# Statistics moved into feed-forward steps, one modulation pass in eight moved from VectorE to ScalarE, and x loaded in two transfers

## The chip, the cores and the metric

The kernel runs on one core of a Trainium2 chip. The metric is the device time of one launch in microseconds, as the median of several runs. The program is one long chain of dense layers for 256 tokens of 1024 features; nothing is shared with another core.

## The reference, cut to what matters

Two blocks of two layers each are applied one after the other. The first block is attention in three branches and a feed-forward part; the second is modulated by a condition vector `c`.

```python
# first block, each of two layers
h = rmsnorm(x, norm_mlp_g[l])
x = x + jnp.square(jax.nn.relu(h @ w_up[l])) @ w_down[l]      # 1024 -> 4096 -> 1024
...
# second block, each of two layers
mod = silu(c) @ ada_w[l] + ada_b[l]                           # 1024 x 9216, one row
sh1, sc1, g1, sh2, sc2, g2, sh3, sc3, g3 = jnp.split(mod, 9, axis=-1)
```

`rmsnorm` divides a row by the root of its mean square. The `mod` row of the second block depends on `c` alone, so it can be computed at any time before that block; the kernel computes it during the feed-forward parts of the first block.

## The kernel before, in words

Every large product is done in fp32 split in two parts: a rounded "high" part and the rest, "low". Three matmuls (lines 603, 604 and 605: high by high, low by high, high by low) make one product. Weights come in chunks of 1 MB (128 x 2048 fp32) from one stream, loaded by SyncE's queue into three raw slots. For each chunk ScalarE writes the high part in two halves (lines 383 and 384) and VectorE the low part in two halves (line 405), into one of two buffers. A raw slot is free again when the low part is done; one of the two split buffers when TensorE has used the chunk before the last.

**Start.** x comes in one transfer. ScalarE squares and sums it in four pieces (line 465), adds EPS (467) and takes ln and exp (469, 470) for each of the two token tiles; VectorE scales x by the result (478), TensorE turns it (491), ScalarE and VectorE make the high and low parts of h (543, 553), and the first product starts. In between the first weight chunk is split, both high halves on ScalarE.

**Feed-forward part of a first-block layer.** There are 16 steps. TensorE runs up0, up1, dn0, up2, dn1, ... (48 matmuls of 256 columns for an up chunk, 24 of 512 columns for a down chunk). In step j ScalarE waits until up j is done, splits the next chunk's high part (dn0 in step 0, up j+1 later), applies relu (1382) and square (1386), splits dn j once dn j-1 is used, copies the hidden rows' high part (696), and issues the two modulation transfers 2j+4 and 2j+5 (`ada_load(j + 2)`, line 1226, 1152 KB each, on ScalarE's own queue). VectorE does the low parts of the same chunks, the hidden rows' low part (702), and two modulation passes, `mac(2j + 2)` and `mac(2j + 3)`. The engines take their instructions strictly in the order written.

**Modulation.** The 1024 x 9216 weight is read as 32 slots (four quarters of 8 slots of 128 x 2304). `mac(i)` multiplies slot i by one condition value per partition and adds it to the quarter's accumulator (1517); the first slot of a quarter (i = 0, 8, 16, 24) writes it instead (1514). Four slot buffers are used in turn. So slot 8 is transferred after step 2 issues it and used by VectorE in step 3, slot 16 is issued in step 6 and slot 24 in step 10.

**Statistics of the second norm.** Since relu and square commute with a positive row scale, the norm's scale is applied only when the feed-forward sum is added to x. The four `norm_square` calls (squares of x in four pieces) stand ahead of step 0 in ScalarE's order; their results are used after step 15.

Of the kernel before, what the change touches and what calls it, by code (L numbers as in the profile page):

```python
# [19 lines left out]
ACT = mybir.ActivationFunctionType  # L20
ALU = mybir.AluOpType
# [4 lines left out]
D = 1024  # L26
# [4 lines left out]
SPLIT = 1024  # L31
# [77 lines left out]
PIECES_OUT = ((0, 0), (1, 0), (0, 1), (1, 1))  # L109
# [107 lines left out]
for _n, _w in (("norm", 24), ("ada_b", MOD), ("dqk", 2), ("dout", 1), ("conv_w", 62), ("conv_b", 2), ("cng", 2), ("cnb", 2), ("fqk", 2)):  # L217
# [14 lines left out]
    "key_rope_ready", "lam_exp", "lam_sum", "latent_rstd", "ln_rstd", "ln_stat", "mac_done", "mix_high", "mix_low",  # L232
    "eps_ready", "softplus_done", "rg_log", "gate_ready", "fgate_log", "conv_log",
    "mla_exp", "mla_masked", "mla_p", "mla_rope_ready", "mla_top", "mods_ready", "o_ready", "o_sq", "p_ready",
# [6 lines left out]
class Machine:  # L241


    def __init__(self, nc):
# [29 lines left out]

        self.loaded = [nc.alloc_semaphore(f"input_loaded{i}") for i in range(9)]
        self.raw_full = [nc.alloc_semaphore(f"raw_full{s}") for s in range(RAW)]
# [524 lines left out]
def ada_acc(m, q):  # L801
    return m.work[:, (q % 2) * ADA_W:(q % 2 + 1) * ADA_W]
# [410 lines left out]
def act_layer1(act, m, plan, step, ada):  # L1213
# [10 lines left out]
    def ada_load(j):  # L1224
        for i in (2 * j, 2 * j + 1):
            act.dma_start(ada_slot(m, i), ada[l * 32 + i]).then_inc(m.ada_full[i % 4], 16)

    def g1(name, t):
        at = l * NV1 + VEC1[name][0] + t
        return m.vec1[:, at:at + 1]  # L1230

    if l == 0:
        split_high(act, m, plan, 0)
        act.wait_ge(m.loaded[2], 16)
    norm_high(act, m, plan, 0, "n1", lambda t: g1("mix", t))
    split_high(act, m, plan, 1)
    if l == 0:
# [133 lines left out]
    for t in range(KT):  # L1371
        if t == 4:
            at_event(split_high, act, m, plan, "wc3")
        high_plain(act, m, plan, "n2", t, g1("mlp", t))
    for i in range(4):
        norm_square(act, m, step, 0, PIECES_OUT, i, -1.0)
    for j in range(FF_TILES):
# [15 lines left out]
        if j + 2 < FF_TILES:  # L1393
            act.wait_ge(m["mac_done"], 32 * l + 2 * j + 2)
            ada_load(j + 2)
    split_high(act, m, plan.next, 0)
    for i in range(4):
# [3 lines left out]
def vec_layer1(dve, m, plan, step):  # L1401
# [102 lines left out]
    def mac(i):  # L1504

        q, kt = i // 8, i % 8
        dve.wait_ge(m.ada_full[i % 4], l * 128 + (16 * (i // 4) + 16))
        ck = m.small[:, 32 + kt:33 + kt]
        if kt == 0:
            if q >= 2:  # L1510
                m.wait_full(dve, plan, f"ada{q - 2}")
            elif l > 0:
                dve.wait_ge(m["ada_last"], l)
            dve.tensor_scalar(ada_acc(m, q), ada_slot(m, i), ck, None, ALU.mult).then_inc(m["mac_done"], 1)
        else:
            dve.wait_ge(m["mac_done"], 32 * l + i)
            dve.scalar_tensor_tensor(ada_acc(m, q), ada_slot(m, i), ck, ada_acc(m, q), ALU.mult, ALU.add).then_inc(m["mac_done"], 1)  # L1517

# [1142 lines left out]
def vec_setup(dve, m):  # L2661
    dve.memset(m.small[:, 0:1], EPS).then_inc(m["eps_ready"], 1)
    norm_unit(dve, m, 0, 0)
    norm_unit(dve, m, 0, 1)


# [32 lines left out]
def act_setup(act, m, step):  # L2699
    act.preload_act_table_set("natural_log_exp_and_others")  # L2700
    act.wait_ge(m.loaded[0], 16)
    act.wait_ge(m["eps_ready"], 1)
    for i in range(4):
        norm_square(act, m, step, None, PIECES_DOWN, i)

# [36 lines left out]
def build(nc, x, pos, c, consts, vec1, vec2, final, row2, stream1, stream2, ada, out):  # L2742
    m = Machine(nc)
    with nc.Block() as block:

        @block.sync
        def _(sp):
            for s in range(RAW):
                sp.sem_inc(m.raw_done[s], 2)
            ident, late = P, CONST["freq"][0]  # L2750
            sp.dma_start(m.x[:, :], x).then_inc(m.loaded[0], 16)
            sp.dma_start(m.consts[:, 0:ident], consts[:, 0:ident]).then_inc(m.loaded[1], 16)
            sp.dma_start(m.vec1[:, :], vec1).then_inc(m.loaded[2], 16)
            for plan in PLANS1 + PLANS2:
# [243 lines left out]
```

## Time and profile before

| what | value |
|---|---|
| median of 3 runs | 2006.41 us (2005.88 to 2006.75) |
| profiled execution | 2007.09 us, span 2004.3 us |
| TensorE busy | 1952.3 us, 97% of the span |
| VectorE busy | 1444.8 us, 72% |
| ScalarE busy | 1148.6 us, 57% |
| DMA | 409.55 MB, mean 204 GB/s |
| first modulation pass of a quarter, line 1514 on VectorE | 8 times, 1.416 us each |
| first weight chunk, from issue at 2.31 us to landing | 6.6 us |
| first up2 matmul, second layer | 799.42 us; last up1 matmul starts at 792.44 us |
| first up4 matmul, second layer | 822.01 us |

The span is what the profiler saw of one execution; the execution's own time is 2.8 us longer. Idle time of ScalarE or VectorE costs nothing while TensorE goes on; a time is lost only where TensorE stops.

### The profile page before, as it was taken

To read this page: it belongs to the slowest core of one execution; us is meant where nothing else is said; L and a number is where in the kernel's file an instruction comes from. 1 tells how busy PE (TensorE), PEld (TensorE's weight loads), DVE (VectorE), ACT (ScalarE), POOL (GpSimd) and SP (SyncE) were. 2 spreads that over 40 slices of the span, in tenths; PEclk is the share of its full clock that TensorE was granted. 3 is DMA by queue.
4 is the path that set the end of the run, shared out by engine and by line. 5 is a ranking of instruction groups with operands and counts; after the bars stand their busy time and mean duration, and the time that the engine had idled before them with its cause. 6 is when DMAs were issued, how large, how long until landed. Compare 5 with 4: busy or idle time off the path is not lost.

```text
span 2004.3 us, 33258 instructions
## 1 busy us (share of the span) xinstructions
PE 1952.3 (97%) x13792; PEld 1761.0 (88%) x13792; DVE 1444.8 (72%) x1922; ACT 1148.6 (57%) x1814; POOL 43.4 (2%) x32
## 2 busy tenths in 40 slices
PE   7999999999999999999899999999999999999999
PEld 7898888888989898888799988699989998878998
DVE  5756798888565788988756589765576657977555
ACT  6358845455436865454655566755565556566554
POOL 0100000000010000000000000000000100000000
PEclk9999999999999999999999999999999999999999
DMA  7453378996554356999455542365546554334553
GB/s 275 144 210 107 125 265 326 389 386 245 194 189 149 105 176 267 391 388 374 167 187 189 189 158 96 107 205 185 184 154 213 189 187 151 126 127 151 188 187 126
DMA packets 56164, 409.55 MB, mean 204 GB/s; under 512 B 6608, under 2 KB 6992, under 8 KB 7888
## 3 DMA queue, kind: packets, MB, share of 16 engines
q1 hardware_dynamic: 46512, 330.23, 46.5%
q10 hardware_dynamic: 9504, 77.21, 9.5%
q8 instruction: 109, 1.79, 0.3%
q14 instruction: 39, 0.32, 0.0%
HBM read 406.37 MB, written 1.05 MB: 203 GB/s over the span
## 4 chain that ended last, share of the span: by engine, by line
PE 79%; DVE 14%; ACT 5%; issue 2%; DMA 0%; DVEq 0%; ACTq 0%; SPq 0%
PE bank L603 25%; PE bank L605 24%; PE bank L604 24%; DVE weights_low L405 4%; ACT weights_high L383 1%; DVE work L2417 1%; DVE work L1517 1%; DVE scratch L1445 1%; ACT work L465 1%; PE bank L940 1%; DVE work L566 1%; DVE h_low L572 1%; ACT weights_high L384 0%; DVE work L1607 0%; DVE scratch L1602 0%
## 5 line engine op out<-in xcount | busy, mean ns | idle before, releaser
L405 DVE TENSOR_TENSOR weights_low<-raw_weights,weights_high 128x1024 fp32r<-128x1024 f32 x608 | 728.4, 1237 | 364.2 <-ACT weights_high L383 357.2
L603 PE MATMUL bank<-h_high,weights_high 128*128 128x256 f32 x3024 | 857.7, 284 | 15.0 <-DVE h_low L572 11.1
L605 PE MATMUL bank<-h_high,weights_low 128*128 128x256 f32 x3024 | 845.3, 280 | 0.0
L604 PE MATMUL bank<-h_low,weights_high 128*128 128x256 f32 x3024 | 844.7, 279 | 0.0
L383 ACT ACTIVATE weights_high<-raw_weights 128x1024 fp32r<-128x1024 f32 x296 | 313.4, 1059 | 619.6 <-PE bank L605 587.9
L603 PEld LDWEIGHTS bank<-h_high,weights_high 128*128 128x128 f32 x3024 | 567.9, 188 | 36.7 <-issue 17.0
L604 PEld LDWEIGHTS bank<-h_low,weights_high 128*128 128x128 f32 x3024 | 568.4, 188 | 2.9 <-issue 0.5
L605 PEld LDWEIGHTS bank<-h_high,weights_low 128*128 128x128 f32 x3024 | 568.6, 188 | 0.0
L384 ACT ACTIVATE weights_high<-raw_weights 128x1024 fp32r<-128x1024 f32 x296 | 309.0, 1044 | 0.0
L603 PE MATMUL bank<-weights_high,hidden_high 128*128 128x512 f32 x640 | 254.3, 397 | 5.1 <-DVE work L2491 2.9
L605 PE MATMUL bank<-weights_high,hidden_low 128*128 128x512 f32 x640 | 252.7, 395 | 0.0
L604 PE MATMUL bank<-weights_low,hidden_high 128*128 128x512 f32 x640 | 252.7, 395 | 0.0
L603 PEld LDWEIGHTS bank<-weights_high,hidden_high 128*128 128x128 f32 x640 | 120.0, 188 | 33.4 <-ACT work L2296 3.3
L1517 DVE SCALAR_TENSOR_TENSOR work<-work,small 128x2304 f32<-128x2304 f32 x56 | 146.5, 2616 | 3.5 <-DVE work L1517 0.5
L605 PEld LDWEIGHTS bank<-weights_high,hidden_low 128*128 128x128 f32 x640 | 120.0, 188 | 29.4
L604 PEld LDWEIGHTS bank<-weights_low,hidden_high 128*128 128x128 f32 x640 | 120.0, 188 | 26.1 <-issue 0.5
L603 PE MATMUL bank<-weights_high,h_high 128*128 128x256 f32 (+1 forms) x320 | 102.9, 322 | 1.0 <-DVE h_low L1178 0.7
L604 PE MATMUL bank<-weights_low,h_high 128*128 128x256 f32 (+1 forms) x320 | 100.7, 315 | 0.0
L605 PE MATMUL bank<-weights_high,h_low 128*128 128x256 f32 (+1 forms) x320 | 100.6, 314 | 0.0
L455 DVE SCALAR_TENSOR_TENSOR work<-bank,work 128x512 f32<-128x512 f32 x74 | 51.1, 691 | 31.2 <-ACT work L449 31.2
L603 PEld LDWEIGHTS bank<-weights_high,h_high 128*128 128x128 f32 x320 | 60.6, 189 | 9.3 <-issue 5.2
L605 PEld LDWEIGHTS bank<-weights_high,h_low 128*128 128x128 f32 x320 | 60.8, 190 | 4.4
(304 smaller groups left out, 1880.0 us busy)
## 6 DMA issues: line engine op xcount, KB each, us to landing
raw_weights<-in_stream SPq DMA_DIRECT2D x310, 1024.0 KB, 4.9
work<-in_ada ACTq DMA_DIRECT2D x64, 1152.0 KB, 9.4
consts<-in_consts SPq DMA_DIRECT2D x1, 2048.0 KB, 12.2
work<-in_row ACTq DMA_DIRECT2D x2, 836.0 KB, 5.5
x<-in_x SPq DMA_DIRECT2D x1, 1024.0 KB, 4.9
out_x<-x SPq DMA_DIRECT2D x4, 256.0 KB, 2.0
gain_row<-in_final SPq DMA_DIRECT2D x1, 512.0 KB, 12.8
vec<-in_vec SPq DMA_DIRECT2D x1, 169.0 KB, 12.1
```

Source lines behind the costliest of these rows:

```text
L383: act.activation(high[:, 0:SPLIT], raw[:, 0:SPLIT], ACT.Copy).then_inc(m["high_a"], 1)
L384: act.activation(high[:, SPLIT:CH], raw[:, SPLIT:CH], ACT.Copy).then_inc(m["high_b"], 1)
L405: dve.tensor_tensor(low[:, c], raw[:, c], high[:, c].bitcast(F32), ALU.subtract).then_inc(m.raw_done[plan.index[name] % RAW], 1)
L455: return dve.scalar_tensor_tensor(to, z, 0.0, to, ALU.min, ALU.subtract)
L465: step(act.activation(h_temp(m)[:, c], m.x[:, c], ACT.Square, accum_out=stat(m, tt, 0 if first else 1)))
L566: dve.tensor_scalar(modulated(m, t), z, gain(t), shift(t), ALU.mult, ALU.add).then_inc(m["temp_vec"], 1)
L572: dve.tensor_tensor(m.hL[:, c], modulated(m, t), m.hH[:, c].bitcast(F32), ALU.subtract).then_inc(m["h_ready"], 1)
L603: pe.matmul(out, aH, bH, start=start, stop=False, skip_group_check=True)
L604: pe.matmul(out, aH, bL, start=False, stop=False, skip_group_check=True)
L605: return pe.matmul(out, aL, bH, start=False, stop=stop, skip_group_check=True)
L940: pe.matmul(m.ps[7][r, c:c + 256], v[:, h * 64:h * 64 + 64], a[:, 0:256], start=True, stop=False, skip_group_check=True)
L1517: dve.scalar_tensor_tensor(ada_acc(m, q), ada_slot(m, i), ck, ada_acc(m, q), ALU.mult, ALU.add).then_inc(m["mac_done"], 1)
```

## The change

There are three edits. First, the start: x is loaded as two transfers of 512 KB, one for each token tile, with the identity matrix's transfer between them, and the first high half of the first weight chunk is made by VectorE (line 2683 of the new kernel, a copy) after it has scaled x; ScalarE makes the second half only. Second, the four `norm_square` calls stand at the ends of steps 2, 3, 4 and 5. Third, the writing pass of the quarters 1 to 3 (slots 8, 16 and 24) is made by ScalarE, at the ends of steps 2, 6 and 10, right behind the transfer that it reads; VectorE waits for it and goes on with the next slot.

```diff
+    def mac_first(q):
+        act.wait_ge(m.ada_full[(8 * q) % 4], l * 128 + 16 * (2 * q) + 16)
+        if q >= 2:
+            m.wait_full(act, plan, f"ada{q - 2}")
+        act.activation(ada_acc(m, q), ada_slot(m, 8 * q), ACT.Copy, scale=m.small[:, 32:33]).then_inc(m["mac_first"], 1)
...
     if l == 0:
-        split_high(act, m, plan, 0)
+        m.wait_raw(act, plan, plan.split[0])
+        split_high_half(act, m, plan, 0, 1)
         act.wait_ge(m.loaded[2], 16)
     norm_high(act, m, plan, 0, "n1", lambda t: g1("mix", t))
+    if l == 0:
+        m.wait_split_first(act, plan, plan.split[0])
...
-    for i in range(4):
-        norm_square(act, m, step, 0, PIECES_OUT, i, -1.0)
     for j in range(FF_TILES):
...
             ada_load(j + 2)
+        if 2 <= j < 6:
+            norm_square(act, m, step, 0, PIECES_OUT, j - 2, -1.0)
+        if j % 4 == 2 and j < 12:
+            mac_first(j // 4 + 1)
...
-        if kt == 0:
-            if q >= 2:
-                m.wait_full(dve, plan, f"ada{q - 2}")
-            elif l > 0:
+        if i == 0:
+            if l > 0:
                 dve.wait_ge(m["ada_last"], l)
             dve.tensor_scalar(ada_acc(m, q), ada_slot(m, i), ck, None, ALU.mult).then_inc(m["mac_done"], 1)
+        elif kt == 0:
+            dve.wait_ge(m["mac_first"], 3 * l + q)
         else:
-            dve.wait_ge(m["mac_done"], 32 * l + i)
-            dve.scalar_tensor_tensor(ada_acc(m, q), ada_slot(m, i), ck, ada_acc(m, q), ALU.mult, ALU.add).then_inc(m["mac_done"], 1)
+            if kt > 1 or i == 1:
+                dve.wait_ge(m["mac_done"], 32 * l + i)
+            dve.scalar_tensor_tensor(ada_acc(m, q), ada_slot(m, i), ck, ada_acc(m, q), ALU.mult,
+                                     ALU.add).then_inc(m["mac_done"], 2 if kt == 1 and q > 0 else 1)
...
 def vec_setup(dve, m):
     dve.memset(m.small[:, 0:1], EPS).then_inc(m["eps_ready"], 1)
+    dve.wait_ge(m.loaded[0], 16)
     norm_unit(dve, m, 0, 0)
+    dve.wait_ge(m.loaded[9], 16)
     norm_unit(dve, m, 0, 1)
+    first, name = PLANS1[0], PLANS1[0].split[0]
+    m.wait_raw(dve, first, name)
+    dve.tensor_copy(m.halves(first, name)[0][:, 0:SPLIT], m.raw_slot(first, name)[:, 0:SPLIT]).then_inc(m["high_a"], 1)
...
-            sp.dma_start(m.x[:, :], x).then_inc(m.loaded[0], 16)
+            sp.dma_start(m.x[:, 0:D], x[:, 0:D]).then_inc(m.loaded[0], 16)
             sp.dma_start(m.consts[:, 0:ident], consts[:, 0:ident]).then_inc(m.loaded[1], 16)
+            sp.dma_start(m.x[:, D:2 * D], x[:, D:2 * D]).then_inc(m.loaded[9], 16)
```

ScalarE, first layer, from the transfers that step 2 issues to the first instructions of step 3, before:

```order
L1226 DMA work<-in_ada 128x2304 [waits mac_done]
L1226 DMA work<-in_ada 128x2304
L383 ACTIVATE weights_high<-raw_weights 128x1024 [waits bank_full2,raw_full1]
L384 ACTIVATE weights_high<-raw_weights 128x1024
L1382 ACTIVATE work<-bank 128x512
```

and now, where `ada_full0` is the landing of slot 8:

```order
L1226 DMA work<-in_ada 128x2304 [waits mac_done]
L1226 DMA work<-in_ada 128x2304
L465 ACTIVATE work,small<-x 128x512 [waits x_ready]
L467 ACTIVATE small<-small 128x1 [waits act_step]
L1233 ACTIVATE work<-work,small 128x2304 [waits ada_full0,act_step]
L383 ACTIVATE weights_high<-raw_weights 128x1024 [waits bank_full2,raw_full1]
```

Three instructions stand ahead of the split of up4 (the L383 that waits for up3's bank) that were not there, and the last of them waits for a transfer issued four rows above it.

ScalarE, first layer, between the h parts and step 0, before (the statistics, then the split of dn0):

```order
L543 ACTIVATE h_high<-bank,vec 128x256 [waits bank_full2] x2
L465 ACTIVATE work,small<-x 128x512 [waits x_ready]
L467 ACTIVATE small<-small 128x1 [waits act_step]
L465 ACTIVATE work,small<-x 128x512 [waits x_ready,act_step]
L467 ACTIVATE small<-small 128x1 [waits act_step]
L465 ACTIVATE work,small<-x 128x512 [waits x_ready,act_step]
L469 ACTIVATE small<-small 128x1 [waits act_step]
L470 ACTIVATE small<-small 128x1 [waits act_step]
L465 ACTIVATE work,small<-x 128x512 [waits x_ready]
L469 ACTIVATE small<-small 128x1 [waits act_step]
L470 ACTIVATE small<-small 128x1 [waits act_step]
L383 ACTIVATE weights_high<-raw_weights 128x1024 [waits bank_full3,raw_full2]
```

and now:

```order
L543 ACTIVATE h_high<-bank,vec 128x256 [waits bank_full2] x2
L383 ACTIVATE weights_high<-raw_weights 128x1024 [waits bank_full3,raw_full2]
L384 ACTIVATE weights_high<-raw_weights 128x1024
L1390 ACTIVATE work<-bank 128x512
L1394 ACTIVATE work<-work 128x512 [waits act_freed]
```

The ten instructions of the statistics are gone from this place, and the split of dn0 follows the last h part.

VectorE at the start, now:

```order
L478 TENSOR_SCALAR work<-x,small 128x512 [waits rstd_ready,input_loaded0]
L478 TENSOR_SCALAR work<-x,small 128x512
L478 TENSOR_SCALAR work<-x,small 128x512 [waits rstd_ready,input_loaded9]
L478 TENSOR_SCALAR work<-x,small 128x512
L2683 CAST weights_high<-raw_weights 128x1024 [waits raw_full0]
L405 TENSOR_TENSOR weights_low<-raw_weights,weights_high 128x1024 [waits high_a]
L553 SCALAR_TENSOR_TENSOR h_low<-bank,vec,h_high 128x256 [waits hH_ready,bank_full0,input_loaded2]
```

The CAST is the added row; without it the rows are those of before.

## Rows read from the trace of the kernel before

**Rows 1.** The page's chain that ended last, shares of the span by engine.
```profile
PE 79%; DVE 14%; ACT 5%; issue 2%; DMA 0%; DVEq 0%; ACTq 0%; SPq 0%
```

**Rows 2.** Timeline, all engines, start: start us, duration us, engine, line, operation.
```profile
0.93 0.39 SPq L2751 DMA_DIRECT2D x<-in_x  x1
...
10.26 0.20 ACT L470 ACTIVATE small<-small 128x1 f32<-128x1 f32 x1
...
10.50 0.88 DVE L478 TENSOR_SCALAR work<-x,small 128x512 f32<-128x512 f32 x2 [1.37 <-ACT small L470]
...
11.45 1.23 DVE L405 TENSOR_TENSOR weights_low<-raw_weights,weights_high 128x1024 fp32r<-128x1024 f32 x1
...
13.23 1.66 DVE L553 SCALAR_TENSOR_TENSOR h_low<-bank,vec,h_high 128x256 fp32r<-128x256 f32 x4 [0.56 <-ACT h_high L543]
14.16 0.29 PEld L603 LDWEIGHTS bank<-h_high,weights_high 128*128 128x128 f32 x1 [1.55 <-DVE h_low L553]
...
17.74 0.41 PE L604 MATMUL bank<-h_low,weights_high 128*128 128x256 f32 x1
```

**Rows 3.** The page's DMA issues: count, KB each, median us from issue to landing.
```profile
work<-in_ada ACTq DMA_DIRECT2D x64, 1152.0 KB, 9.4
...
x<-in_x SPq DMA_DIRECT2D x1, 1024.0 KB, 4.9
out_x<-x SPq DMA_DIRECT2D x4, 256.0 KB, 2.0
```

**Rows 4.** Timeline of TensorE, first layer, feed-forward steps 1 to 3.
```profile
313.92 0.28 PE L605 MATMUL bank<-h_high,weights_low 128*128 128x256 f32 x1
...
321.17 0.36 PE L603 MATMUL bank<-h_high,weights_high 128*128 128x256 f32 x1 [0.62 <-DVE weights_low L405]
...
338.16 0.40 PE L603 MATMUL bank<-weights_high,hidden_high 128*128 128x512 f32 x1
...
343.76 0.28 PE L603 MATMUL bank<-h_high,weights_high 128*128 128x256 f32 x1
```

**Rows 5.** Timeline of ScalarE, first layer, feed-forward steps 0 and 3.
```profile
310.11 1.04 ACT L383 ACTIVATE weights_high<-raw_weights 128x1024 fp32r<-128x1024 f32 x1
...
338.44 1.06 ACT L383 ACTIVATE weights_high<-raw_weights 128x1024 fp32r<-128x1024 f32 x1 [3.13 <-PE bank L605]
```

**Rows 6.** Timeline of VectorE, first layer, feed-forward steps 0 and 1.
```profile
311.26 2.36 DVE L405 TENSOR_TENSOR weights_low<-raw_weights,weights_high 128x1024 fp32r<-128x1024 f32 x2 [3.40 <-ACT weights_high L383]
...
314.56 5.33 DVE L1517 SCALAR_TENSOR_TENSOR work<-work,small 128x2304 f32<-128x2304 f32 x2
319.81 4.62 DVE L405 TENSOR_TENSOR weights_low<-raw_weights,weights_high 128x1024 fp32r<-128x1024 f32 x4
```

**Rows 7.** Line 1226, step 2 of the first layer: the pair's issues and landings.
```profile
L1226 ACTq DMA_DIRECT2D work<-in_ada x2: 334/395/456, 332.9 to 333.3; - x2
...
DMA to landing us min/median/max: 8.6/10.7/12.8
```

**Rows 8.** The page's groups of ScalarE copies: busy us, mean ns of one.
```profile
L384 ACT ACTIVATE weights_high<-raw_weights 128x1024 fp32r<-128x1024 f32 x296 | 309.0, 1044 | 0.0
```

**Rows 9.** ScalarE's groups by shape: busy us, mean ns.
```profile
L696 ACT ACTIVATE hidden_high<-work 128x512 fp32r<-128x512 f32 x76 | 46.8, 616 | 0.1
```

**Rows 10.** Line 1226, step 2 of the second layer.
```profile
L1226 ACTq DMA_DIRECT2D work<-in_ada x2: 335/395/455, 811.2 to 811.5; - x2
...
DMA to landing us min/median/max: 8.4/10.6/12.7
```

**Rows 11.** Line 1226, step 6 of the first layer.
```profile
L1226 ACTq DMA_DIRECT2D work<-in_ada x2: 334/395/456, 379.2 to 379.6; - x2
...
DMA to landing us min/median/max: 6.8/9.3/11.7
```

**Rows 12.** Timeline of TensorE, first layer: the first matmul of up8.
```profile
390.36 0.28 PE L603 MATMUL bank<-h_high,weights_high 128*128 128x256 f32 x1
```

**Rows 13.** Busy time by stretch: PE, PEld, DVE, ACT, POOL, PEclk, DMA share, GB/s.
```profile
324.00:468.00 144.00, 143.93 (x948) 126.85 (x947) 125.81 (x92) 69.60 (x86) 0.00 (x0) 1.00 0.97 388
```

More of the change, by code:

```diff
@@ L232 @@
     "key_rope_ready", "lam_exp", "lam_sum", "latent_rstd", "ln_rstd", "ln_stat", "mac_done", "mix_high", "mix_low",
-    "eps_ready", "softplus_done", "rg_log", "gate_ready", "fgate_log", "conv_log",
+    "eps_ready", "mac_first", "softplus_done", "rg_log", "gate_ready", "fgate_log", "conv_log",
     "mla_exp", "mla_masked", "mla_p", "mla_rope_ready", "mla_top", "mods_ready", "o_ready", "o_sq", "p_ready",
@@ L272, in __init__ @@
         self.ps = [nc.alloc_psum_tensor(f"bank{b}", [P, 512], F32) for b in range(8)]
-        self.loaded = [nc.alloc_semaphore(f"input_loaded{i}") for i in range(9)]
+        self.loaded = [nc.alloc_semaphore(f"input_loaded{i}") for i in range(10)]
         self.raw_full = [nc.alloc_semaphore(f"raw_full{s}") for s in range(RAW)]
@@ L2703, in act_setup @@
     for i in range(4):
+        if i == 2:
+            act.wait_ge(m.loaded[9], 16)
         norm_square(act, m, step, None, PIECES_DOWN, i)
```

## The prediction

> **What bounds the kernel now.** I read the chain of waits first. It gives TensorE 79% of the span and VectorE 14% [rows 1], so a gain has to come from a place where TensorE stands still, and a loss arises where a new wait reaches it. The timeline of TensorE shows two such places beside the change. At the start it has nothing to do with products until 14.16 [rows 2]. In the feed-forward part of the first layer it ends up1 at 313.92 + 0.12 = 314.04, and starts up2 only at 321.17, released by VectorE's low part [rows 4]. An undisturbed down chunk takes 343.76 - 338.16 = 5.60, and up4 follows dn2 there without a gap [rows 4]. The reader is to see that in step 3 there is no wait to remove, but a seam that can open. The third view is the pair of transfers that each step issues: it lands 8.6 us or more after its issue in step 2 [rows 7], in a stretch where the DMA engines are busy 0.97 of the time [rows 13].
>
> **The statistics leave the place before step 0.** Before, ScalarE started the split of dn0 at 310.11 [rows 5], straight behind the four squares. Its own release is the end of up0. An up chunk takes 5.65 (ScalarE's step of 11.25 less 5.60), so up1 began near 308.4, and ScalarE starts 0.28 after such a seam (338.44 against 338.16, [rows 4, 5]): 308.7. ScalarE, and VectorE behind it, come 1.4 earlier. VectorE's passes stand from 314.56 to 319.81, then the low part of up2, and TensorE follows 321.17 - 319.81 = 1.36 later [rows 4, 6]. Now that is 318.4 + 1.36 = 319.8; TensorE itself would be ready at 314.04 + 5.60 = 319.64. up2 starts at 319.8 instead of 321.17: 1.4 gained. The second layer has the same seam, up1 ending at 792.56 and up2 starting at 799.42. TensorE is ready at 798.16, so at most 1.26 is gained, and VectorE is advanced by about as much. Together **-2.65**. Once VectorE is earlier, the next thing late is TensorE's own dn0.
>
> The squares themselves land in steps 2 to 5. One piece with its small operations is about 1.2 us (four took the 4.5 us between the h parts and 310.11) and ScalarE idled 3.13 before step 3's split [rows 5]. They cost nothing in steps 3 to 5. In step 2 they are covered by the wait that comes next.
>
> **The writing pass on ScalarE.** VectorE loses six passes of 1.416 us, in steps 3, 7 and 11. TensorE did not wait for VectorE in these steps (up4 followed dn2 without a gap), so this saves nothing. What the pass costs on ScalarE has no row of its size. From 128x512 in 0.616 to 128x1024 in 1.044 [rows 8, 9] is 0.84 ns an element, and 1.044 + 1280 x 0.00084 = 2.1; in proportion to the larger one it would be 2.25 x 1.044 = 2.35, and at the rate of the slope alone 1.9. I take 2.1, by the row nearest in size, and keep 1.9 to 2.35.
>
> More important is when it can start. It waits for slot 8, whose transfer is issued four rows earlier, and the split of up4 is queued behind it on ScalarE. For that split VectorE's low part waits, and for that TensorE. In the first layer the pair is issued at 332.9 and the first of it lands 8.6 later, at 341.5 [rows 7]. The pass then runs to 343.65. The split of up4, which started at 338.44, starts there. From the start of a high half to VectorE's low half is 311.26 - 310.11 = 1.15 [rows 5, 6], from there to TensorE 1.36. TensorE gets up4 at 343.65 + 2.5 = 346.15 instead of 343.76: **+2.4**. All this moves as a whole by the 1.4 gained before. In the second layer the issue at 811.2 and the landing 8.4 later [rows 10] give 819.6 + 2.1 + 2.5 = 824.2 against 822.01: **+2.2**.
>
> In step 6 the pair is issued at 379.2 and slot 16 lands 6.8 later, at 386.0 [rows 11]; 386.0 + 2.1 + 2.5 = 390.6 against 390.36 [rows 12]: **+0.3**. Step 6 of the second layer and step 10 of both have landings of 5.2 to 6.6, and come out at or before TensorE's own time: 0. The transfers that step 3 issues go out later by what TensorE was held, and they are used later by as much, so I count nothing more. Sum of the waits: **+4.9**.
>
> On these transfers the Trainium skill (DMA: Bandwidth & Descriptors, Issuing engines are not separate DMA queues) says that transfers started by different engines share the same 16 DMA engines and interleave. The trace agrees: 1152 KB need 8.6 us here. This page speaks against the third edit, as ScalarE's own queue gives the slot no right of way over the weights.
>
> **The start.** x in one piece lands 4.9 after its issue, 256 KB of the output take 2.0 [rows 3]. Between them, 512 KB would take 2.97, which is 1.9 less; at the rate of the busiest stretches, about 430 GB/s, half of x is 1.2 less. I take 1.4. ScalarE needs the second half 2.4 us after its start, when by its place in the queue it has landed. Everything down to VectorE's second scaling then moves from 10.50 to 9.1. ScalarE then makes one weight half instead of two and is no longer last; VectorE is, as it has the copy too. Its low half started at 11.45 and the first low part of h at 13.23, 0.56 of that waiting for ScalarE [rows 2]. This wait goes, and the copy comes in. The copy has no row of its own. The scaling of 128x512 takes 0.44 of VectorE's time (0.88 for two), the subtraction of the same 128x1024 takes 1.23 [rows 2]. At twice the scaling less one start it is about 0.7, at the subtraction 1.2. With 0.7, VectorE's first low part starts at 13.23 - 1.4 + (0.7 - 0.56) = 12.0, TensorE gains about 1.3; with 1.2 it gains 0.8. I take 0.7 since it too reads one tensor: **-1.3**. Bounds 0.5 and 1.9. The first weight chunk lands at 2.31 + 6.6 = 8.9, in time for either.
>
> For the copy the Trainium skill (VectorE: DVE Perf Modes, The perf-mode tier table) says that fp32 copies and tensor-scalar operations in SBUF run at twice the rate of an fp32 operation on two tensors. The scaling rows agree; that it holds for a copy with a rounded output no row of before shows. By the rule the start gives -1.3, by the subtraction's row -0.8.
>
> **The sum.** -2.65 + 4.9 - 1.3 = +0.95 against the profiled execution's 2007.09, which is 2008.0. The median of the runs is 2006.41, 0.68 lower, so the forecast for it is 2007.4, which is no change: a measurement of this kernel can tell about 0.2%, 4 us, from nothing.
>
> **The rivals.**
>
> *Slow landings.* The slot lands as late in steps 6 and 10 as the median of all 64 transfers, 9.4 us [rows 3]. For: the median itself, and a DMA share of 0.97 [rows 13]. Against: the pair's second half makes that median, the first one came after 5.2 to 8.6 in all six places. Its place is ScalarE before the split of up8 and up12. Price at 9.4: step 2 costs 3.2 in each layer, and the four others about 2.8 each (379.2 + 9.4 + 4.6 = 393.2 against 390.36). That is 6.4 + 11.2 = 17.6, less 2.65 and 1.3: +13.7, or 2020. It decides from landings of 7.4 in the four later places on: then these cost 4 x 0.8 = 3.2, the waits are 4.6 + 3.2 = 7.8, and the sum is 7.8 - 3.95 = +3.9, or 2010.3.
>
> *No wait at all.* If the slot lands within 6.2 us of its issue in step 2, as it does in later steps, the pass ends in ScalarE's idle time. For: 5.2 to 6.8 elsewhere. Against: 8.6 and 8.4 at the very place [rows 7, 10]. Then -2.65 - 1.3 = -3.95, or 2002.4.
>
> *The start gives little.* Either TensorE's clock rises at the same time as before, or the copy is slow. Until 17.74 a matmul of 256 columns is shown with 0.41 [rows 2], later with 0.28 [rows 4], starting 0.21 and 0.12 apart: TensorE is at its 1.2 GHz level at first and then at 2.4. If it rises at the same time, half of the 1.3 is lost. Result 2006.41 + 0.95 + 0.65 = 2008.0.
>
> *VectorE sets the end of a step.* If the six passes taken from VectorE were on its path after all, 6 x 1.416 = 8.5 would be gained, or 1999. Only steps 3, 7 and 11 could show it, and TensorE's seams there are closed before. I give it almost nothing.
>
> **How the numbers follow.** The forecast 50%, the start giving little 19%, slow landings 17% (half of them between 2010 and 2012), no wait 12%, VectorE 2%. The predicted time is 2007.4. The no-wait case lies on the edge of what can be told; with the larger start gain of 1.9 it is beyond it, and I count 9 of its 12 as faster, with VectorE's 2. The range reaches into the no-wait case down to 2003.0, and into slow landings up to 2011.5 (7.7 us in the later places). Faster than 2002.4: 11%; slower than 2010.4: 17%; in between 72%.
>
> **What would show it.** Right: TensorE reaches the first product at about 12.9; up2 follows dn0 without a gap in both layers; in step 2 ScalarE sits idle for some 4 to 5 us ahead of the 128x2304 pass, released by the transfer, and TensorE then waits about 2.3 us before up4, released by VectorE's low part; before up8 and up12 it waits 0.3 or less. Wrong: no such wait before up4; the wait before up8 or up12 over 1 us; a stop before dn4 or later for a transfer that step 3 issued late; or a start that comes no earlier.

## The result, and the profile after

The changed kernel takes 2012.94 us in the median (2007.05 to 2019.46, 16 runs) against 2006.58 (2003.70 to 2009.13, 16 runs) for the kernel before on the same chip. The ratio is 1.0033, 95% interval 1.0023 to 1.0043: some 6.6 us slower, above the forecast's range of 2003.0 to 2011.5. The 16 runs lie in two groups of eight, 2007.05 to 2011.47 and 2014.41 to 2019.46, and the median falls between them. The profiled execution took 2017.55 us with a span of 2015.4, so it is one of the slower ones; a second profiled execution of the same kernel took 2012.71 (below, changed again).

The page's chain of waits gives TensorE 77% instead of 79% [rows 1], and the DMAs, which had 0%, now hold 3%:

```profile
PE 77%; DVE 13%; ACT 4%; DMA 3%; issue 2%; SPq 0%; DVEq 0%; ACTq 0%
```

**Statistics.** The timeline of TensorE at up2, first layer (start us, duration us, then engine, line and operation), answers to [rows 4]:

```profile
317.74 0.40 PE L605 MATMUL bank<-weights_high,hidden_low 128*128 128x512 f32 x1
318.08 0.36 PE L603 MATMUL bank<-h_high,weights_high 128*128 128x256 f32 x1
```

The gap before up2 is gone. A seam is the place where one chunk's matmuls end and the next chunk's begin. "Cost at a seam" means, all along this document, how much further one matmul lags behind its twin in the trace of before than the matmul ahead of it did. From the last matmul of up1 to the first of up2 it was 321.17 - 313.92 = 7.25 before; now up1's last starts at 312.26, and it is 318.08 - 312.26 = 5.82. TensorE gains 1.43, and in the second layer 0.95.

**The writing pass.** ScalarE between steps 2 and 3, first layer, same columns; in brackets its idle time before an instruction and what ended it. The L1226 row is the issue of the two transfers:

```profile
330.10 1.06 ACT L383 ACTIVATE weights_high<-raw_weights 128x1024 fp32r<-128x1024 f32 x1 [2.85 <-DMA raw_weights<-in_stream]
330.19 0.82 ACTq L1226 DMA_DIRECT2D work<-in_ada  x2
...
333.27 0.29 ACT L467 ACTIVATE small<-small 128x1 f32<-128x1 f32 x1
339.53 2.22 ACT L1233 ACTIVATE work<-work,small 128x2304 f32<-128x2304 f32 x1 [5.96 <-DMA work<-in_ada]
341.66 1.04 ACT L383 ACTIVATE weights_high<-raw_weights 128x1024 fp32r<-128x1024 f32 x1
```

and line 1226 there, which answers to [rows 7]:

```profile
DMA to landing us min/median/max: 9.3/11.8/14.3
```

The pass takes 2.22, within the 1.9 to 2.35 that was kept for it. The slot lands 9.3 after its issue, not 8.6. TensorE, in the same place:

```profile
340.43 0.40 PE L605 MATMUL bank<-weights_high,hidden_low 128*128 128x512 f32 x1
344.17 0.36 PE L603 MATMUL bank<-h_high,weights_high 128*128 128x256 f32 x1 [3.34 <-ACT work L1390]
344.36 0.28 PE L604 MATMUL bank<-h_low,weights_high 128*128 128x256 f32 x1
344.48 0.28 PE L605 MATMUL bank<-h_high,weights_low 128*128 128x256 f32 x1
...
345.74 0.42 PE L603 MATMUL bank<-h_high,weights_high 128*128 128x256 f32 x1
345.96 0.42 PE L604 MATMUL bank<-h_low,weights_high 128*128 128x256 f32 x1
...
348.92 0.28 PE L603 MATMUL bank<-h_high,weights_high 128*128 128x256 f32 x1
349.04 0.28 PE L604 MATMUL bank<-h_low,weights_high 128*128 128x256 f32 x1
```

Read the starts, not the durations. The stop before up4 costs 3.50. The profile says that ScalarE's relu of up3's bank ended it (L1390, at 344.12); VectorE's first low half of up4, begun at 342.80, ends within 0.2 of that, and behind the stop of up8 it is the one that is named. Then the matmuls start 0.12 apart, from 345.53 to 348.74 they start 0.21 apart, and after that 0.12 again. In 3.4 us TensorE does 16 matmuls where 0.117 each would have taken 1.9: **1.5 us more, behind the stop**. The view of busy time by stretch shows why (its column after POOL is the granted clock, then DMA share and GB/s):

```profile
344.20:348.70 4.50, 4.50 (x26) 4.50 (x27) 3.89 (x5) 3.91 (x7) 0.00 (x0) 0.64 0.65 215
...
395.30:399.80 4.50, 4.50 (x26) 4.50 (x27) 3.89 (x5) 3.01 (x4) 0.00 (x0) 0.65 0.67 227
```

The granted clock is 0.64 there and was 1.00 before the stop: TensorE falls from its 2.4 GHz level to the 1.2 GHz level for some 3.4 us. The second of these rows is up8. There ScalarE's pass, whose landing answers to [rows 11]:

```profile
390.64 2.22 ACT L1233 ACTIVATE work<-work,small 128x2304 f32<-128x2304 f32 x1 [7.26 <-DMA work<-in_ada]
```

and TensorE, the first matmul of up8 answering to [rows 12]:

```profile
391.89 0.40 PE L605 MATMUL bank<-weights_high,hidden_low 128*128 128x512 f32 x1
395.28 0.36 PE L603 MATMUL bank<-h_high,weights_high 128*128 128x256 f32 x1 [3.00 <-DVE weights_low L405]
```

The slot, issued at 381.0, landed 9.6 later instead of the 6.8 of before. The stop costs 3.1 and the slow matmuls 1.6. Before up4 of the second layer the stop is 3.2 and the slow matmuls 1.5; up8 there costs nothing, up12 0 in the first layer and 0.3 in the second. So three seams cost 5.0 + 4.7 + 4.7 = 14.4, where the forecast had 4.9 in all.

**The start**, all engines, answers to [rows 2]:

```profile
4.55 0.63 ACT L465 ACTIVATE work<-x 128x512 f32<-128x512 f32 x1 [2.53 <-DMA x<-in_x]
7.28 0.63 ACT L465 ACTIVATE work<-x 128x512 f32<-128x512 f32 x1 [0.36 <-DMA x<-in_x]
9.75 0.88 DVE L478 TENSOR_SCALAR work<-x,small 128x512 f32<-128x512 f32 x2 [1.84 <-ACT small L470]
10.55 0.69 DVE L2683 CAST weights_high<-raw_weights 128x1024 fp32r<-128x1024 f32 x1
12.41 1.65 DVE L553 SCALAR_TENSOR_TENSOR h_low<-bank,vec,h_high 128x256 fp32r<-128x256 f32 x4
13.34 0.58 PE L603 MATMUL bank<-h_high,weights_high 128*128 128x256 f32 x1 [1.08 <-DVE h_low L553]
```

The first product comes 0.82 earlier. The copy costs 0.69, as chosen. But ScalarE waits 0.36 for the second half of x, and VectorE's second scaling moves only from 10.50 to 9.75. TensorE's first matmuls start 0.21 apart and later ones 0.12. Once both kernels are at 0.12, from 17.77 on, the gain is 0.66. The moment of this rise is not the same in every execution. In the second profiled execution of the changed kernel the first product is 0.70 earlier than in the trace of before and only 0.16 is left after the rise; in the kernel without the third edit 0.81 and 0.07. With the start of before unaltered (the statistics alone, the third edit alone) the rise came so early that those two executions were 1.8 ahead of the trace of before.

### The profile page after: what moved, and what is told of

Read it like the earlier page. It is cut to its first block, busy times and chain, and to the rows that moved or that the text cites. A ratio compares the mean times of both kernels' runs of the same rounds, so it can differ in the third digit from the quotient of the medians.

```text
span 2015.4 us, 33268 instructions
## 1 busy us (share of the span) xinstructions
PE 1954.8 (97%) x13792; PEld 1762.4 (87%) x13792; DVE 1436.6 (71%) x1917; ACT 1160.4 (58%) x1819; POOL 41.1 (2%) x32
## 4 chain that ended last, share of the span: by engine, by line
PE 77%; DVE 13%; ACT 4%; DMA 3%; issue 2%; SPq 0%; DVEq 0%; ACTq 0%
PE bank L603 24%; PE bank L605 24%; PE bank L604 23%; DVE weights_low L405 4%; DMA work<-in_ada 1%; ACT weights_high L383 1%; DMA raw_weights<-in_stream 1%; DVE work L2431 1%; DVE scratch L1457 1%; DVE work L1530 1%; PE bank L940 1%; DVE work L566 1%; DVE h_low L572 1%; DVE work L1621 0%; DVE scratch L1616 0%
## 5 line engine op out<-in xcount | busy, mean ns | idle before, releaser
L383 ACT ACTIVATE weights_high<-raw_weights 128x1024 fp32r<-128x1024 f32 x295 | 312.1, 1058 | 586.9 <-PE bank L605 553.6
```

Of the source, the lines that this page charges most:

```text
L383: act.activation(high[:, 0:SPLIT], raw[:, 0:SPLIT], ACT.Copy).then_inc(m["high_a"], 1)
```

## The experiments

Several accounts stood against each other. Mine: the third edit alone is the loss, through a stop that the late slot and the pass make together, and through the fall of the clock behind it. The rivals: that the other two edits do harm, that one half of the third suffices, or that the slow matmuls come from data that arrive slowly. Each ratio is to the kernel before on the same chip.

**Without the third edit.** VectorE's line 1514 makes all eight passes again, and `mac_first` is gone:

```diff
-        if j % 4 == 2 and j < 12:
-            mac_first(j // 4 + 1)
```

> The changed kernel with the writing pass back on VectorE (third edit undone; the start and the moved statistics stay). Theory A, the writing pass on ScalarE is the whole loss: it holds ScalarE until slot 8 has landed, TensorE stops about 3 us before up4 in each layer and sometimes before up8, and after such a stop it runs at its lower clock for some 4 us, which costs 1.5 us more. Then this kernel is 2 to 4 us faster than before (2002.5 to 2004.5) and its trace has no stop over 1 us before up4 or up8. Rival B, the moved statistics disturb steps 2 to 5: it stays 2 us or more slower than before. Rival C, the shifted start puts the DMA queues in a worse phase: no faster than before, with late landings.

Measured: 2003.48 (12 runs), ratio 0.9987 (0.9977 to 0.9996), so neither of the other two edits makes the loss. The last matmul of dn2 and the first of up4:

```profile
341.01 0.40 PE L605 MATMUL bank<-weights_high,hidden_low 128*128 128x512 f32 x1
341.24 0.28 PE L603 MATMUL bank<-h_high,weights_high 128*128 128x256 f32 x1
```

No stop. Up4 of the second layer costs 0.55.

**The third edit alone**, added to the kernel before.

> The kernel before with the third edit alone (writing pass of slots 8, 16, 24 on ScalarE). Theory A: 6 to 12 us slower than before (2012 to 2018), with stops of 2 to 3.5 us before up4 in both layers and slow matmuls behind those of 3 us and more. Rival B or C: within 2 us of before.

Measured: 2016.15 (7 runs), ratio 1.0041 (1.0026 to 1.0056). With the first run this puts the loss on the third edit. Its runs too lie in two groups, 2011.01 to 2012.19 and 2016.15 to 2016.69. Its first up4:

```profile
342.70 0.36 PE L603 MATMUL bank<-h_high,weights_high 128*128 128x256 f32 x1 [1.85 <-ACT work L1389]
...
343.77 0.41 PE L604 MATMUL bank<-h_low,weights_high 128*128 128x256 f32 x1
343.98 0.41 PE L605 MATMUL bank<-h_high,weights_low 128*128 128x256 f32 x1
```

The stops cost 2.0 and 2.2, and the clock falls behind both (+1.6, +1.5), where I had expected it behind stops of 3 and more only. Without the other two edits the stop is the 2.4 and 2.2 that I had worked out, or less.

**The pass one step later**, behind the square of steps 3, 7 and 11 of the changed kernel:

```diff
         act.activation(hidden(m, j), relu_temp(m, j), ACT.Square).then_inc(m["u_ready"], 1)
+        if j % 4 == 3 and j < 12:
+            mac_first(j // 4 + 1)
...
-        if j % 4 == 2 and j < 12:
-            mac_first(j // 4 + 1)
```

> The changed kernel with the writing pass on ScalarE one step later, behind the square of steps 3, 7 and 11, when ScalarE has already split the next up chunk. The pass is the same, only the wait for the landing no longer stands ahead of the split. Theory A: no stop before up4 and up8; 2 to 4 us faster than before, as without the pass on ScalarE (2002.5 to 2004.5). Rival D, the pass itself (2.2 us of ScalarE) or VectorE's wait for it is the cost: 4 us or more slower than that, 2007 or more.

Measured: 2003.77 (12 runs), ratio 0.9990 (0.9979 to 1.0001). ScalarE:

```profile
340.54 2.23 ACT L1233 ACTIVATE work<-work,small 128x2304 f32<-128x2304 f32 x1 [0.52 <-DMA work<-in_ada]
```

The same pass on the same engine costs TensorE nothing at the first layer's up4 and up8 and 0.65 at the second layer's up4. The place makes the loss.

**The wait alone**, on the kernel without the third edit: ScalarE waits for slots 8, 16 and 24 at the old place and does nothing with them.

```diff
+        if j % 4 == 2 and j < 12:
+            act.wait_ge(m.ada_full[0], l * 128 + 16 * (j + 2) // 2 + 16)
```

> The variant without the pass on ScalarE, but ScalarE still waits at the ends of steps 2, 6 and 10 until slot 8, 16 or 24 has landed; VectorE makes the pass. Theory A: the stop before up4 is that of the changed kernel less the pass, 3.3 - 2.1 = 1.2 us in both layers, without a fall of the clock; 2 to 4 us slower than the variant without pass (2005.5 to 2007.5). Rival F, the wait is nothing and the 2.2 us pass is what costs: as the variant without pass, 2003.5.

Measured: 2005.0 (11 runs), ratio 0.9989 (0.9980 to 0.9998). Up4 costs 0.1 in the first layer and 0.2 in the second. That is a miss: I had expected a stop of 1.2. In this execution the slot landed 8.3 after its issue; at the 9.3 of the changed kernel the wait would reach 1.0 further, and no trace of this kernel shows what that costs.

**The pass without the wait**, on the same kernel:

```diff
+        if j % 4 == 2 and j < 12:
+            step(act.activation(h_temp(m), m.x[:, :], ACT.Copy))
```

> The variant without the pass on ScalarE, but with a plain copy of 128x2048 on ScalarE at the ends of steps 2, 6 and 10 whose input has long been there (nothing reads it); VectorE makes the pass. Theory A: ScalarE idles over 3 us there, so no stop of TensorE and the same time as the variant without pass, within 1 us (2003.5). Rival F, the pass is what costs: 2 us or more slower.

The copy is 128x2048 and takes 1.94, a little less than the pass. Measured: 2004.26 (11 runs), ratio 0.9992 (0.9983 to 1.0001). No seam costs over 0.3. So in these executions ScalarE's idle time covers the wait alone, and it covers the work alone; one behind the other they are not covered.

**The start alone**, added to the kernel before.

> The kernel before with the new start alone. Theory A: the first product starts 0.6 to 0.9 us earlier as in the changed kernel, and this shift is still there at the end: 0 to 1.5 us faster than before, not to be told from no change. Rival G, the rest of the start is bound by the transfers or the clock: the shift is gone by 20 us.

Measured: 2007.77 (11 runs), ratio 1.0007 (0.9998 to 1.0016). The first product is at 13.59, 0.57 earlier, and 0.39 of it is left once the matmuls start 0.12 apart. The rival that nothing is left is not what this trace shows, but the time doesn't show a gain either.

**The statistics alone**, added to the kernel before.

> Before with the second edit alone: the four pieces of the statistics stand in steps 2 to 5, everything else is as before. By my term, up2 starts 1.3 to 1.4 us earlier in each layer and nothing else changes: 2.4 to 2.7 us less than before, ratio 0.9987. The rival that the chain absorbs it (VectorE's modulation passes set up2's low part anyway, so the split being earlier only lengthens a wait) gives no change, ratio 1.000. The rival that the squares in step 2 to 5 hold the next split of ScalarE gives a stop before up4 and a ratio above 1.

Measured: 2005.39 (11 runs), ratio 0.9985 (0.9976 to 0.9993). From up1's last matmul to up2's first TensorE gains 1.43 in the first layer and 1.15 in the second; up4 gives 0.36 and 0.14 back. Of the three edits alone, the product 0.9985 x 1.0007 x 1.0041 is 1.0033, the ratio of the whole; with intervals of 0.001 or so on each side, an agreement this close is partly chance.

**Stops of chosen length.** To the kernel before, unread copies of x on ScalarE at the ends of steps 2, 4, ... 12, longer from seam to seam in the first layer, shorter in the second. All transfers are there in time.

```diff
+        if j in DELAY[l]:
+            for n in DELAY[l][j]:
+                step(act.activation(h_temp(m)[:, 0:n], m.x[:, 0:n], ACT.Copy))
```

> The kernel before, with plain copies of x into a free scratch region added on ScalarE at the ends of steps 2, 4, 6, 8, 10 and 12 (nothing reads them), so long that TensorE should stop before the next up chunk for about 1.0, 1.5, 2.0, 2.5, 3.0 and 3.5 us, in this order in the first layer and in the reverse in the second. No transfer is waited for. Theory A with the clock: behind the long stops matmuls of 256 columns start 0.21 us apart for some 4 us, behind the short ones 0.12 from the first on; the changed kernel shows the fall after 3.3 us and the start of the second block shows none after 1.4, so the border lies between; it need not be sharp. Rival E, the slow matmuls come from late data: none of the twelve is followed by slow matmuls, as all its data are there.

One run, 2030.57. Cost of the stops at up4 to up14: 1.0, 0.8, 1.3, 1.6, 2.6, 2.7 in the first layer, none followed by slow matmuls; 3.5, 2.1, 2.5, 0.6, 1.1, 0.3 in the second, the first two followed by them (+1.6, +1.5). TensorE after the 3.5 and after the 2.1:

```profile
836.10 0.36 PE L603 MATMUL bank<-h_high,weights_high 128*128 128x256 f32 x1 [3.35 <-ACT work L1383]
...
863.53 0.35 PE L603 MATMUL bank<-h_high,weights_high 128*128 128x256 f32 x1 [1.84 <-ACT work L1383]
```

and the stretches behind these two and behind the 2.5:

```profile
836.10:840.50 4.40, 4.40 (x25) 4.40 (x26) 3.79 (x4) 3.04 (x4) 0.00 (x0) 0.64 0.58 203
...
863.60:868.00 4.40, 4.40 (x25) 4.40 (x26) 3.79 (x4) 2.97 (x4) 0.00 (x0) 0.62 0.65 226
...
890.20:894.60 4.40, 4.40 (x38) 4.40 (x39) 3.79 (x4) 2.97 (x4) 0.00 (x0) 1.00 0.66 216
```

With no late data the clock still falls, so slow data are not the cause. The border isn't sharp: the clock fell behind 2.1 and did not behind 2.5, 2.6 and 2.7. It is one execution.

**TensorE kept busy in the stop.** To the changed kernel, 26 matmuls (3.1 us) before up4 and up8 of both layers, into a bank that is overwritten.

```diff
+FILL = 26
...
+        if j in (4, 8):
+            pe_begin(pe, m, plan, f"up{j}")
+            for _ in range(FILL):
+                pe.matmul(m.bank(plan, f"up{j}")[:, 0:T], m.hH[:, 0:P], m.hH[:, 0:T], start=True, stop=True, skip_group_check=True)
```

> The changed kernel with 26 matmuls of 256 columns put into the seam before up4 and before up8 in both layers (about 3 us each; their result is overwritten). They need nothing that is late, so TensorE stays busy while it waits for the split. Theory A with the clock: the matmuls behind the seam before up4 start 0.12 us apart from the first on, and each stop of 3 us and more costs 1.5 us less than in the changed kernel, while a seam without a stop (up8 of the second layer) costs up to 3 us more: 0 to 4 us faster than the changed kernel's 2012.9 in all. Rival E, the slow matmuls behind the seam come from the data (the split arrives late in both halves) and not from the stop: they stay 0.21 us apart and nothing is gained.

Measured: 2016.58 (6 runs), ratio 1.0053 (1.0037 to 1.0069): a miss. The trace tells the two halves apart:

```profile
342.42 3.27 PE L1094 MATMUL bank<-h_high 128*128 128x256 f32 x26
345.92 0.36 PE L603 MATMUL bank<-h_high,weights_high 128*128 128x256 f32 x1 [0.23 <-ACT work L1395]
346.11 0.28 PE L604 MATMUL bank<-h_low,weights_high 128*128 128x256 f32 x1
346.23 0.28 PE L605 MATMUL bank<-h_high,weights_low 128*128 128x256 f32 x1
```

The clock stays up, but the fill costs its 3.1 also where there would have been no stop: up8 costs 3.1 in both layers, though slot 16 landed 5.3 after its issue in the first. A shorter one follows: 16 matmuls, before up4 of both layers and up8 of the first. Against the kernel just shown:

```diff
-FILL = 26
+FILL = 16
...
-        if j in (4, 8):
+        if j == 4 or (j == 8 and l == 0):
```

> The changed kernel with 16 matmuls of 256 columns, some 1.9 us, in front of up4 in both layers and of up8 in the first layer, where TensorE stands still for about 3.3 us. They write a bank that up4 or up8 overwrites, and run in time in which TensorE has nothing to do. If the clock's fall after a stop is what costs 1.5 us at each place, the rest of the stop is 1.4 us, the clock stays at its upper level, and the kernel is 3 to 4.5 us faster than the changed one: about 2008.5, ratio to before 1.001. If the filling takes as long as it gives (because it starts later than the stop does, as in the kernel with 26), the time is that of the changed kernel or above it, ratio 1.003 to 1.005. If the slow matmuls come from the work behind the stop and not from the stop, they stay, and the time is the changed kernel's.

Measured: 2012.67 (10 runs), ratio 1.0026 (1.0016 to 1.0035), which doesn't part from the changed kernel: a miss, as about 2008.5 was expected. The clock doesn't fall at the filled seams, where up4 costs 2.7 and 2.2. Up8's fill costs 1.9, since the slot landed 5.1 after its issue there and nothing would have stopped, and up12 of the second layer has a stop of 2.4 with a fall behind it (+1.6), as slot 24 landed 8.8 after its issue.

**The changed kernel again**, unaltered, one profiled run.

> The changed kernel once more, unaltered, for a second look at its three places. By the landings of the first look (9.3 and 9.6 us in steps 2 and 6) the stops are about 3.3 us each; if the landings scatter between executions, steps 2 and 6 land between 6.8 and 9.6, the stop before up4 lies between 2.2 and 3.5 and that before up8 between 0.3 and 3.2, and slow matmuls follow only where the stop is above about 2 us. A time between 2007 and 2019 is what either gives.

It took 2012.71. First-layer up4:

```profile
346.23 0.40 PE L603 MATMUL bank<-h_high,weights_high 128*128 128x256 f32 x1 [3.73 <-ACT work L1390]
346.43 0.41 PE L604 MATMUL bank<-h_low,weights_high 128*128 128x256 f32 x1
346.64 0.41 PE L605 MATMUL bank<-h_high,weights_low 128*128 128x256 f32 x1
```

and ScalarE's pass of step 6:

```profile
388.57 2.23 ACT L1233 ACTIVATE work<-work,small 128x2304 f32<-128x2304 f32 x1 [2.88 <-DMA work<-in_ada]
```

Up4 costs 3.9 + 1.55 and, in the second layer, 2.7 + 1.5. Up8 costs nothing: the pair was issued at 383.3, and the slot landed within 5.3. So up4 stops in both executions, and up8 (4.7) comes and goes with a landing.

**Fill before up4 alone**, 16 matmuls in both layers. Against the kernel with the short fill:

```diff
-        if j == 4 or (j == 8 and l == 0):
+        if j == 4:
```

> The changed kernel with 16 matmuls of 256 columns in front of up4 alone, in both layers; in front of up8 there are none, since the slot sometimes lands early there and the fill would then cost its 2 us. If the clock's fall is an additional 1.5 us at each up4, up4 costs about 2.7 and 2.2 us against before instead of 5.4 and 4.2, no 256-column matmul behind up4 starts 0.21 us after the one before it, and the kernel takes 3 to 4.5 us less than the changed one: ratio to before 1.0010 to 1.0020. If the fall costs nothing in the end, the ratio stays at 1.0033.

Measured: 2009.05 (12 runs), ratio 1.0006 (0.9997 to 1.0014), apart from the changed kernel's 1.0023 to 1.0043 and better than the 1.0010 to 1.0020 expected. Up4 costs 2.6 and 2.2:

```profile
341.35 2.07 PE L1094 MATMUL bank<-h_high 128*128 128x256 f32 x16
343.92 0.35 PE L603 MATMUL bank<-h_high,weights_high 128*128 128x256 f32 x1 [0.49 <-ACT work L1395]
344.11 0.28 PE L604 MATMUL bank<-h_low,weights_high 128*128 128x256 f32 x1
```

The stretch behind the stop, busy time, granted clock, DMA share:

```profile
344.20:348.70 4.50, 4.50 (x40) 4.50 (x39) 3.89 (x5) 3.66 (x7) 0.00 (x0) 1.00 0.72 235
```

In 4.5 us behind the stop, at a granted clock of 1.00, 40 matmuls are shown where the changed kernel has 26. Matmuls that compute nothing won back some 5 us by the ratios, of which the two falls are 3. The rest is within the intervals and the scatter of landings: in this execution the slot landed 8.6 after its issue and up8 did not stop, so the stops at up4 are shorter than the changed kernel's too (2.6 and 2.2 against 3.5 and 3.2, or 3.9 and 2.7).

## Why the prediction was wrong

**Statistics: right.** -2.65 forecast; -2.4 in the first profile (1.43 + 0.95) and -2.6 in the second, and the ratio of the edit alone, 0.9985, is -3.0 (-4.8 to -1.4).

**The writing pass: mechanism and duration right.** 2.1 was taken, 2.22 measured. ScalarE sat idle 5.96 for the slot, one more than my 4 to 5. From the end of the pass to TensorE it is 344.17 - 341.75 = 2.4, against my 2.5. That VectorE's six passes bring nothing held too: with the pass one step later on ScalarE the ratio is 0.9990, with all passes on VectorE 0.9987.

**"The first of it lands 8.6 later" and "all this moves as a whole by the 1.4 gained before": the stop at up4 was undersized.** With the third edit alone the stops cost 2.0 and 2.2, against my +2.4 and +2.2. In the changed kernel they cost 3.5 and 3.2 in one execution, 3.9 and 2.7 in the other: some 2 us more than the 4.6 of my sum. How far the pass's start lies behind up2's start decides it. In my sum this was 341.5 - 321.17 = 20.3. In the first layer it was 20.0 in the kernel with the third edit alone (stop 2.0), 20.5 and 20.7 in the kernels with 16 matmuls of fill (2.6, 2.7), 339.53 - 318.08 = 21.45 in the changed kernel (3.5) and 21.85 in its second execution (3.9): the stop is this distance less 18.0. Of the 1.15 that my distance lacked, 0.7 is the landing (9.3 for 8.6) and 0.4 the issue, which came 12.1 behind up2's start where it had come 11.7. ScalarE waits for the weights just before it, 2.85 (2.44 in the kernel before), in a stretch where the DMA engines were already busy 0.97 [rows 13]. Why the slot landed late in both executions of the changed kernel stays open: the kernels with 16 matmuls of fill have the same gain ahead of up2, the slot landed 8.6 after its issue in them, and their stops are within 0.4 of my +2.4 and +2.2; in the one with 26 it landed at 9.4. Over all profiled executions slot 8 of the first layer landed 7.8 to 9.4 after its issue.

**"Step 6: +0.3": true of one execution, wrong of another.** The landing of 6.8 that I read is one draw. In the profiled executions of the kernels here slot 16 landed between 5.0 and 9.6 after its issue. At 9.6 the seam cost 3.1 + 1.6. My rival of slow landings had this place and this price (2.8 at 9.4), and I gave it 17% on the ground that the first of each pair had come sooner in six places, all of them of one execution.

**The term that was missing: the clock behind a stop.** This is the step that failed. The sum of the waits, +4.9, ended with the stop itself. Each stop of 2.0 to 3.9 that the pass made in a kernel without fill was followed by 16 matmuls at the 1.2 GHz level, +1.5. Two at up4 make 3.0, up8 adds 1.6 when it stops. I had read both spacings, 0.21 and 0.12, at the start [rows 2, 4], and used them for the start alone. The trace of before even had such a fall behind a stop, late in the second block, and the prediction made no use of it. TensorE there waits 1.89, starts again at 1767.73, and its next 256-column matmuls are 0.21 apart; the granted clock is 0.83 over ten us (the last row, busy time by stretch):

```profile
1767.73 0.49 PE L2020 MATMUL bank<-work 64*128 64x128 f32 x4 [1.89 <-ACT scratch L2290]
...
1770.76 0.41 PE L603 MATMUL bank<-weights_high,h_high 128*128 128x256 f32 x1
1770.97 0.41 PE L604 MATMUL bank<-weights_low,h_high 128*128 128x256 f32 x1
...
1766.00:1776.00 10.00, 7.15 (x45) 6.61 (x45) 9.14 (x19) 8.41 (x19) 0.00 (x0) 0.83 0.30 107
```

The Trainium skill (TensorE: Matmul & The Clock Gate, HAM oscillation — how this bites in real kernels) says that TensorE's waits for data between groups of products can let its clock fall, so that each next group starts slow. The traces agree, 0.64 granted behind the stop, and the kernel with chosen stops shows that the wait need not be for data.

Made up anew, with the second profiled execution: start -0.2 (0.70 at the first product, 0.16 with the clock up), statistics -1.4 and -1.2, up4 +5.4 and +4.2, up8 0. That is +6.8; its span is 2010.9 - 2004.3 = 6.6 longer than that of before. Against the forecast's +0.95 it is some 6 more: 3.0 from the two falls, 2.0 from the two stops and 1.1 from the start, less 0.3 at up8. That the medians differ by 6.4 as well is partly luck, since the changed kernel's median lies in the gap between two groups of runs. Where slot 16 is late, up8 adds 4.7, which is a likely reason for the slower group; the groups lie about 7 apart, though, and no trace shows the rest.

**The start: mis-sized.** -1.3 forecast; -0.8 and -0.7 at the first product in the two executions of the changed kernel, and -0.66 and -0.16 once the clock is up; -0.57 and -0.39 in the kernel with the start alone. The copy was right (0.69 for 0.7). What failed is "ScalarE needs the second half 2.4 us after its start, when by its place in the queue it has landed": it waited 0.36 for it. The rival "the start gives little" was the truer one here, and for the reason it gave: the moment of the clock's rise moves by more between executions than the edit gains.

The best version of those run is the one without the third edit, 0.9987 (0.9977 to 0.9996), with the statistics alone as good at 0.9985 (0.9976 to 0.9993): both are a little faster than the kernel before, and what the traces show of that is the statistics.

## What to carry to other kernels

A stop of TensorE can have two prices: its length, and the slow matmuls behind it. In this kernel the second, 1.5 us, came with every stop over 3 us and with some of about 2 us. Look in the trace of before for a stop of that length and read the starts behind it. Before an engine gets both a wait and new work in front of a split that TensorE needs, compare the two together with its idle time: each alone was covered here, their sum wasn't, and one step later it was again. A landing in a stretch where the DMA engines are full is a draw; take the spread from several places and executions, and don't let it move along with a gain elsewhere.

## What the runs showed that I had not expected

- A stop behind which the clock falls costs 1.5 us more than its length, since some 3.4 us are then run at the 1.2 GHz level. The fall came with the first matmul after the stop, or up to 1.4 us later (345.53 after 344.17). At these seams none of the stops up to 1.6 had it; of those of 2.0 to 2.7 some did and some did not, and of those of 3.1 and more all did.
- The column of the granted clock reads 1.00 in the first 18 us of the trace of before, though its matmuls start 0.21 apart until 18.17. There only the starts show the lower level.
- The moment of the first rise moved the whole execution by up to 1.8 us between kernels with the same start.
- Matmuls without use in the stop kept the granted clock at 1.00.
- The copy of 128x1024 with rounded output took VectorE 0.69, the subtraction of the same size 1.23.
- Transfers of 1152 KB in the same step landed 5.0 to 9.6 us after issue from one kernel's execution to the next.
